# Sums of squares added elementwise first, key squares in column groups, split products for the values, and a shared key copy in a two-layer hybrid decoder step

## What is computed

```python
cq, ckv, kr = split(rms_norm(x, norm_g) @ w_in)        # 512 | 256 | 32 channels
q = rms_norm((rms_norm(cq, q_a_norm) @ w_uq).reshape(B, T, 16, 96), q_norm)
c = rms_norm(ckv, kv_a_norm)
k_nope = einsum('btc,chd->bthd', c, w_uk)              # 16 heads x 64
ssq = sum(square(k_nope), -1) + sum(kr * kr, -1)[..., None]
inv_r = rsqrt(ssq / 96 + EPS)                          # a scale per token and head
v = einsum('btc,chv->bthv', c, w_uv)                   # 16 heads x 64
```

## Time and profile before

| | |
|---|---|
| median of three executions | 1514.9 us |
| lowest, highest | 1511.93 us, 2867.42 us |
| span of the profiled execution | 1503.7 us |
| TensorE busy in it | 1457.7 us (97%) |
| VectorE, ScalarE, GpSimd busy | 756.1, 595.4, 162.6 us |

### The profile page before, as it was taken

The page is one execution under the profiler, slowest core; times in us unless marked ns, Lnnn a source line. Parts: engine busy times, 40 slices in busy tenths (PEclk is TensorE's granted clock), DMA queues, the critical chain, the costliest instruction groups (busy, mean ns, idle before and its releaser), DMA issues.

```text
span 1503.7 us, 29069 instructions
## 1 busy us (share of the span) xinstructions
PE 1457.7 (97%) x11768; PEld 1366.1 (91%) x11768; DVE 756.1 (50%) x1284; ACT 595.4 (40%) x909; POOL 162.6 (11%) x194
## 2 busy tenths in 40 slices
PE   7999988889999999999999999999999999999999
PEld 6999988877999999999999967655799999999999
DVE  6887555667964444443323327566444444443222
ACT  5444532334344344332223364567434434432111
POOL 1000022211810000000100000452020000000000
PEclk9999999999999999999999999999999999999999
DMA  5222200003452232333333420465323222333232
GB/s 216 85 84 84 85 1 29 29 29 105 148 193 95 88 94 84 98 88 103 101 91 90 113 85 29 144 195 167 115 85 94 89 96 86 87 94 91 88 91 81
DMA packets 48575, 144.64 MB, mean 96 GB/s; under 512 B 6912, under 2 KB 16224, under 8 KB 47344
## 3 DMA queue, kind: packets, MB, share of 16 engines
q1 hardware_dynamic: 42048, 118.57, 25.4%
q0 software_dynamic: 6160, 20.79, 4.6%
q10 hardware_dynamic: 288, 4.19, 0.7%
HBM read 134.73 MB, written 7.76 MB: 95 GB/s over the span
## 4 chain that ended last, share of the span: by engine, by line
PE 86%; DVE 7%; issue 3%; ACT 2%; DVEq 0%; DMA 0%; ACTq 0%; POOLq 0%
PE PS L561 85%; DVE arena L1837 2%; ACT arena L1633 1%; PE PS L1094 1%; DVE arena L2000 1%; DVE mx L2275 1%; DVE arena L1827 0%; DVE arena L1832 0%; ACT wsplit L1276 0%; DVE arena L2052 0%; DVE wsplit L1739 0%; DMA gains<-in_gains 0%; DVE arena L1835 0%; ACT arena L1455 0%; DVE arena L2027 0%
## 5 line engine op out<-in xcount | busy, mean ns | idle before, releaser
L561 PE MATMUL PS<-xnh,wsplit 128*128 128x260 f32 x3904 | 636.8, 284 | 12.6 <-DVE wsplit L1739 12.6
L561 PEld LDWEIGHTS PS<-xnh,wsplit 128*128 128x128 f32 x3904 | 539.5, 189 | 15.1 <-DVE wsplit L1739 13.2
L561 PE MATMUL PS<-xnl,wsplit 128*128 128x260 f32 x1952 | 393.7, 283 | 0.0
L1276 ACT ACTIVATE wsplit<-wring 128x1024 fp32r<-128x1024 f32 x176 | 183.0, 1040 | 438.1 <-PE PS L561 434.8
L1739 DVE TENSOR_TENSOR wsplit<-wring,wsplit 128x1024 fp32r<-128x1024 f32 x176 | 211.0, 1199 | 207.1 <-ACT wsplit L1276 207.0
L561 PEld LDWEIGHTS PS<-xnl,wsplit 128*128 128x128 f32 x1952 | 301.2, 189 | 0.0
L561 PE MATMUL PS<-hidh,wsplit 128*128 128x260 f32 x1408 | 226.6, 283 | 0.0
L561 PEld LDWEIGHTS PS<-hidh,wsplit 128*128 128x128 f32 x1408 | 192.9, 188 | 0.0
L561 PE MATMUL PS<-arena 128*128 128x128 f32 (+9 forms) x1104 | 170.9, 322 | 13.1 <-DVE arena L2000 8.6
L561 PEld LDWEIGHTS PS<-arena 128*128 128x128 f32 (+2 forms) x1104 | 134.3, 191 | 48.2 <-issue 30.1
L561 PE MATMUL PS<-hidl,wsplit 128*128 128x260 f32 x704 | 141.3, 282 | 0.0
(11 more groups left out here) (411 smaller groups left out, 1649.9 us busy)
## 6 DMA issues: line engine op xcount, KB each, us to landing
wring<-in_w_gu SPq DMA_DIRECT2D x88, 512.0 KB, 3.6
wring<-in_w_dn SPq DMA_DIRECT2D x32, 512.0 KB, 3.5
wring<-in_w_proj SPq DMA_DIRECT2D x28, 512.0 KB, 3.6
wring<-in_w_dn SPq DMA_DIRECT2D x16, 384.0 KB, 3.1
wring<-in_w_outa SPq DMA_DIRECT2D x8, 512.0 KB, 4.1
wring<-in_w_inc SPq DMA_DIRECT2D x8, 512.0 KB, 3.6
wring<-in_w_uq SPq DMA_DIRECT2D x8, 512.0 KB, 4.9
wring<-in_w_outc SPq DMA_DIRECT2D x8, 512.0 KB, 3.9
```

Source lines behind the costliest of these rows:

```text
L561: return pe.matmul(out, lhsT, rhs, start=start, stop=stop)
L1276: act.activation(dst[:, 0:w], wring[slot(stage, u)][:, 0:w], ACT.Copy).then_inc(s('w_hi'), 1)
```

## The change

- **Norms:** all eight squares of a norm are added elementwise; `norm_sum` has one `both`. The eighth add is GpSimd's in norms 1 to 3. In norm 0 it is VectorE's, behind `low('proj', 0, 1)`.
- **Latent squares:** VectorE adds the two squares of the keys' latent, GpSimd the four of the queries' (`add_latent`), and TensorE sums over partitions once for each group. The sum for the queries moves to behind key tile 2.
- **Key squares:** ScalarE's squares of four tiles are kept in four buffers. `key_squares(t)` sums each of the four into its own group of 32 PSUM partitions, after tile 5 (t=0) and after tile 7 (t=1). The sum is copied to `sq` by ScalarE and gathered to 16 rows by one more `both`, after the second value output; the key's root moves there too.
- **Values:** their weights are split (high part on GpSimd, remainder on VectorE behind the last key copy) and they are computed in 48 fp32r products of 512 columns.
- **Key copies:** VectorE copies the odd head of each key tile (`key_copy`), and ScalarE waits for that copy before it squares the tile and copies the even head.

```diff
-            for k in range(first, KD - 1):
+            for k in range(first, KD):
                 add_square(n, k)
...
             pool.dma_start(O['rows_c'], clat).then_inc(s('out_stored'), 16)
+            add_latent(2)
+            add_latent(3)
             pool.wait_ge(s('rot_ready'), 5)
...
+            add_latent(4)
+            add_latent(5)
+            for k in range(2):
+                pool.wait_ge(w_loaded[k], 16 * (GBASE['uq'] + 1))
+                pool.tensor_copy(uvh[:, k, :], wring[k][:, :]).then_inc(s('rest_hi'), 1)
...
+            pool.wait_ge(s('v_mm'), 8)
             pool.dma_start(wukt, A['w_ukt']).then_inc(g_loaded, 16)
...
-                pe.wait_ge(s('sq_added'), (KD - 1) * (n + 1))
-                both(4, const('ones_d'), sqsum, True, False)
-                pe.wait_ge(s('sq_ready'), KD * (n + 1))
-                both(4, const('ones_d'), sq[:, 1, :], False, True).then_inc(s('ssq_mm'), 1)
+                pe.wait_ge(s('sq_added'), squares_before(n) + KD)
+                both(4, const('ones_d'), sqsum).then_inc(s('ssq_mm'), 1)
...
-            mean_square(0)
-            mean_square(1)
+            pe.wait_ge(s('sq_added'), KD * 3 + 1)
+            both(4, const('ones_256'), sq[:, 0, :]).then_inc(s('latent_mm'), 1)
             latent_tile(3)
...
             latent_tile(4)
-            pe.wait_ge(s('rot_ready'), 4)
-            mean_square(2)
-            mean_square(3)
             latent_tile(5)
...
+            def key_squares(t):
+                pe.wait_ge(s('kn_sq'), 4 * t + 4)
+                for half in range(2):
+                    for g in range(4):
+                        ins = mm(PS[32 * g:32 * g + 32, 4 + half, 0:HALF], const('keysel')[:, 32 * t:32 * t + 32],
+                                 squares[g][:, half * HALF:(half + 1) * HALF], t == 0, t == 1)
+                ins.then_inc(s('kn_mm'), 1)
...
-                if m == 0:
-                    mean_square(4)
-                if m == 1:
-                    mean_square(5)
-                if m >= 1:
-                    key_square(m - 1)
-            key_square(7)
+                if m == 2:
+                    pe.wait_ge(s('rot_ready'), 4)
+                    pe.wait_ge(s('sq_added'), KD * 3 + 5)
+                    both(6, const('ones_512'), sqsum).then_inc(s('latent_mm'), 1)
+                if m == 5:
+                    key_squares(0)
+            key_squares(1)
...
+            pe.wait_ge(s('rest_split'), 3)
...
-                    ins = mm(PS[:, 6 + n % 2, :], clat[:, k, (n // 2) * 128:(n // 2 + 1) * 128],
-                             wring[k][:, (n % 2) * 512:(n % 2 + 1) * 512], k == 0, k == 1)
+                    mm(PS[:, 6 + n % 2, :], clh[:, k, toks], uvh[:, k, ns_], k == 0, False)
+                    mm(PS[:, 6 + n % 2, :], cll[:, k, toks], uvh[:, k, ns_], False, False)
+                    ins = mm(PS[:, 6 + n % 2, :], clh[:, k, toks], uvl[:, k, ns_], False, k == 1)
...
+                if n == 1:
+                    pe.wait_ge(s('kn_sq'), 9)
+                    both(4, const('keysel')[:, 64:64 + MH], sq[:, 0, :], True, False)
+                    pe.wait_ge(s('c_hi'), 1)
+                    both(4, const('ones_96')[0:32, 0:16], krsq, False, True).then_inc(s('kn_mm'), 1)
...
             def key_tile(m):
...
-                act.wait_ge(*((s('kn_mm'), m - 1) if m >= 2 else (s('cq_mm'), 5 + m)))
-                act.activation(two(sq[:, p, :]), bank2(2 * p), ACT.Square).then_inc(s('kn_sq'), 1)
-                for e in range(2):
...
+                act.wait_ge(*((s('kn_mm'), 1) if m >= 4 else (s('rot_ready'), 5) if m >= 2 else (s('sq_added'), KD * 3 + 4 + m)))
+                act.wait_ge(s('key_copied'), m + 1)
+                act.activation(two(squares[m % 4]), bank2(2 * p), ACT.Square).then_inc(s('kn_sq'), 1)
+                act.activation(two(khat[0:64, 2 * m, :]), PS[0:64, 2 * p:2 * p + 2, 0:HALF], ACT.Copy).then_inc(tile_taken[p], 1)
             for m in range(8):
                 key_tile(m)
-                if m == 1:
-                    act.wait_ge(s('cq_mm'), 6)
+                if m == 2:
+                    act.wait_ge(s('latent_mm'), 4)
                     rsqrt(R_CQ, two(rinv[:, R_CQ % 2, :]), bank2(6))
-                if 3 <= m <= 6:
-                    act.wait_ge(s('c_norm'), m)
-                    act.activation(cqh[:, m - 3, :], cqraw[:, m - 3, :], ACT.Copy).then_inc(s('c_hi'), 1)
+                if m >= 4:
+                    act.wait_ge(s('c_norm'), m - 1)
+                    act.activation(cqh[:, m - 4, :], cqraw[:, m - 4, :], ACT.Copy).then_inc(s('c_hi'), 1)
...
             low('proj', 0, 1)
+            square_added(KD - 1)
...
+            for m in range(3):
+                key_copy(m)
             dve.wait_ge(s('rinv_ready'), R_CQ + 1)
             for j in range(4):
+                key_copy(3 + j)
                 st(stt(out=cqraw[:, j, :], in0=cqraw[:, j, :], scalar=small[:, C_QA + j:C_QA + j + 1], in1=rinv[:, R_CQ % 2, :],
                        op0=ALU.mult, op1=ALU.mult), s('c_norm'))
                 if j:
                     latent_low(j + 1)
                 if j >= 2:
                     low('uq', 0, j)
+            key_copy(7)
+            for k in range(2):
+                dve.wait_ge(s('rest_hi'), 2 + k)
+                st(tt(uvl[:, k, :], wring[k][:, :], uvh[:, k, :].bitcast(F32), ALU.subtract), s('rest_split'))
             latent_low(5)
```

More of the change, by code:

```diff
@@ L74 @@
 CONSTS = ['ident', 'triu', 'decaymask', 'causal', 'ones', 'ones_d', 'ones_128', 'ones_256', 'ones_512',
-          'ones_96', 'rot128', 'sel4', 'headsel'] + [f'inv{l}' for l in range(LV + 1)]
+          'ones_96', 'rot128', 'sel4', 'keysel'] + [f'inv{l}' for l in range(LV + 1)]
 C_GDN, C_D, C_SSM, C_QA, C_KVA, C_QN, C_QR, C_KR, C_KN, C_EPS, C_QK, NSMALL = 0, 1, 5, 9, 13, 15, 16, 17, 18, 19, 20, 21
@@ L342, in s, with squares_before @@
             return sems[name]
+        def squares_before(n):
+            return KD * n + (5 if n == 3 else 0)
         def slot_freed(stage, i, u):
@@ L470, in add_square, with add_latent @@
                 else:
-                    pool.wait_ge(s('sq_added'), (KD - 1) * n + k)
+                    pool.wait_ge(s('sq_added'), squares_before(n) + k)
                     pool.tensor_tensor(sqsum[:, :], sqsum[:, :], sq[:, k % 2, :], ALU.add).then_inc(s('sq_added'), 1)
             def sum_squares(n, first=0):
-                for k in range(first, KD - 1):
+                for k in range(first, KD):
                     add_square(n, k)
+            def add_latent(j):
+                pool.wait_ge(s('cq_sq'), j + 1)
+                if j == 2:
+                    pool.tensor_copy(sqsum[:, :], sq[:, 0, :]).then_inc(s('sq_added'), 1)
+                else:
+                    pool.wait_ge(s('sq_added'), KD * 3 + j - 1)
+                    pool.tensor_tensor(sqsum[:, :], sqsum[:, :], sq[:, j % 2, :], ALU.add).then_inc(s('sq_added'), 1)
             pool.memset(raw[:, 0, 0:3], 0.0)
@@ L940, in latent_tile @@
                 ins.then_inc(gemm_ready[p], 1)
[L942 to L946, removed]
             latent_tile(0)
@@ L970, in _ @@
             pe.wait_ge(s('ln_ready'), R_KV + 1)
-            def key_square(m):
-                pe.wait_ge(s('kn_sq'), m + 1)
-                both(4, const('headsel')[:, m * 16:(m + 1) * 16], sq[:, m % 2, :], m == 0, False).then_inc(s('kn_mm'), 1)
+            def key_squares(t):
[5 more added lines that the diff above has]
+                ins.then_inc(s('kn_mm'), 1)
             for m in range(8):
@@ L980, in _ @@
                 ins.then_inc(gemm_ready[p], 1)
-                if m == 0:
-                    mean_square(4)
-                if m == 1:
-                    mean_square(5)
-                if m >= 1:
-                    key_square(m - 1)
-            key_square(7)
-            pe.wait_ge(s('c_hi'), 1)
-            both(4, const('ones_96')[0:32, 0:16], krsq, False, True).then_inc(s('kn_mm'), 1)
-            for u in range(2):
-                pe.wait_ge(w_loaded[u], 16 * (GBASE['uq'] + 1))
+                if m == 2:
[6 more added lines that the diff above has]
+            pe.wait_ge(s('rest_split'), 3)
             pe.wait_ge(s('ln_ready'), R_CQ + 1)
@@ L1529, in latent_square @@
                 if j >= 2:
-                    act.wait_ge(s('cq_mm'), j - 1)
+                    act.wait_ge(*((s('latent_mm'), 2) if j < 4 else (s('sq_added'), KD * 3 + j - 2)))
                 src = clat[:, j, :] if j < 2 else cqraw[:, j - 2, :]
@@ L1588, in _ @@
                 if t < 4:
-                    act.wait_ge(*((s('kn_mm'), 8) if t < 2 else (s('rot_ready'), 5)))
+                    act.wait_ge(s('kn_mm'), 3)
                 else:
@@ L2169, in _ @@
             latent_out(1)
-            dve.wait_ge(s('kr_mm'), 1)
+            dve.wait_ge(s('cq_sq'), 2)
+            st(tt(sq[:, 0, :], sq[:, 0, :], sq[:, 1, :], ALU.add), s('sq_added'))
+            dve.wait_ge(s('latent_mm'), 1)
```

(12 more changed lines are left out.)

35 lines of the change are left out of this document (20 added, 15 removed).

## The result

The changed kernel takes **1513.47 us** in the median (1504.72 to 1515.84, 20 runs), the kernel before on the same chip 1507.36 us (20 runs from 1504.05, with one of 2867). The ratio is 1.0026, 95% interval 1.0013 to 1.0038: slightly slower, well within 2%. The first three times of before gave 11.2 us between span and run; 20 runs show 1.7 (a run of 1515.35 us had a span of 1513.6). Against the kernel before I had forecast -1.4 us, and it is about +3.9 (0.26%).

The account below looks back on a forecast made before the run. TensorE was taken as the bound, with ScalarE also nearly full in the key phase. Norm 0 +1.25, norms 1 and 3 -1.74, norm 2 to queries -0.87 gave -1.4: span 1502.3 plus 11.2, 1513.5 us; 8-in-10 range 1506 to 1519.

Parts of the forecast that it names:

- the sum: Whole kernel: norm 0 +1.25, norms 1 and 3 -1.74, norm 2 to the queries -0.87, together -1.4 us.
- Norm 0: Norm before the convolution: VectorE's eighth add waits behind a weight remainder, so TensorE goes on later, +1.25 us.
- Norms 1 and 3: Each loses one `both` of 0.87 us, with GpSimd's eighth add covered: -1.74 us together.
- norm 2 and the single latent sum: Norm 2 loses one `both`, and the keys' latent pair of sums becomes one: -0.87 us each.
- Norm 2 to the queries: Norm 2 through key phase and values: earlier savings mostly eaten by the key-phase chain, -0.87 us left.
- The walk: Key-phase queues followed tile by tile: VectorE and ScalarE tied together, TensorE idle, values start at 881.3 against 880.99.
- The copy at 0.70 us: Key phase: VectorE's 64x520 copy out of PSUM priced at 0.70 us, with 0.42 as the other end.
- Values: 48 fp32r products of 512 columns at 0.225 us each; phase ends at 894.1 against 894.99.
- A: Rival: TensorE sets the pace and the saving shows in full, -14.2 us, 1500.7; chance 0.12.
- B: Rival: split-value products take 0.34 us each, costing more than plain ones, +4.0 us, 1518.9; chance 0.13.
- C: Rival: GpSimd operations around key phase and norms hold up VectorE's, +2.8 us, 1516.3; chance 0.10.
- Span to run time: Whole kernel: 11.2 us added between the profile's span of 1502.3 and the median run time.

Follow-up runs that it names:

- e1: Changed kernel with norm 0 alone summed as before the change (seven adds on VectorE, two sums on TensorE): 1511.53 us, ratio to before 1.0023.
- e9: e6 with the values in plain fp32 as before, without the rounded copies and remainders: 1505.52 us.
- e4: Changed kernel with VectorE's key-phase queue reordered, key copies and value-weight remainders earlier, same instructions: 1503.09 us, ratio to before 0.9967.
- e6: Changed kernel with e1 and e4 together: 1499.33 us, ratio to before 0.9946.
- e2: Changed kernel with 14 unread fp32 products of 260 columns filling TensorE's key-phase idle ahead of the second key_squares: 1509.79 us, ratio to before 1.0011.
- e10: e2 plus 16 unread products of 128 columns in norm 0's wait, so both new idles are filled: 1512.35 us.
- e5: Changed kernel with 26 unread products of 256 columns laid between the thin ones at the start of attention: 1511.14 us, ratio to before 1.0018.
- the series: Kernel before with 2, 4, 8, 12 or 20 unread products of 260 columns ahead of the values: 1509.96, 1513.59, 1510.99, 1514.67, 1517.34 us.
- e8: e6 with six unread dense products at the start of attention: 1499.68 us, ratio to before 0.9937.
- e13: Kernel before with 20 unread products of 260 columns ahead of the values: 1517.34 us.

## Why the prediction failed

- **Direction, wrong: -1.4 forecast, +3.9 measured.** The step that failed is the sum: it priced TensorE's idle by its length alone and carried no term for the granted clock. The first paragraph read that clock as at the upper level "in nearly every slice" and then left it out. What the runs show in its place: work -2.8, low clock +6.4. What the change moves was right to about 1 us a part, and the low clock outweighed it.
- **Norm 0, +1.25:** right as work (1.26, e1). The total at 151 us is +3.04; the missing 1.8 is the clock after the idle.
- **Norms 1 and 3, -1.74:** -0.93 and -0.86, right; norm 2 and the single latent sum, -0.73 and -0.79 against 0.87 each.
- **Norm 2 to the queries, -0.87:** measured +0.2 (from +1.67 to +1.88). The walk gave the tile times to within 1 us, shifted by the 1.67 us that after is late at norm 1: key phase from 854.93 (walk 853.2, shifted 854.9), last copy at 878.93 (walk 879.9). It was 0.9 too late at that copy, and 1.8 short of the low clock behind it (0.8 in the key squares, 1.0 in the first value products). The copy at 0.70 us is exact. What the prediction took from the Trainium skill, "VectorE: DVE Perf Modes", section "Why PSUM operands drop a tier", that an fp32 operand in PSUM keeps VectorE at its plain rate, agrees with it: 0.70 us for 520 columns out of PSUM, where the copy within SBUF took 0.42.
- **Values:** 0.2315 us for a product against 0.225; 11.1 against 14.0 us in all, confirmed by e9.
- **Everything behind the queries** stood in the sum as unchanged, without a word. It is the largest error of the profiled run: +7.3 us at the start of attention and +1.55 by 1090, all of it clock.
- **Rivals:** A did not happen as run, but e4 and e6 show that most of it was there behind VectorE's order (work -9.0 for e6). B is refuted. C's mechanism is there once, off the chain. Beside a GpSimd add of 1.75 us, VectorE's line 2212 took 1.69 us, where the same operation in the kernel before, with GpSimd at rest, took 0.69. GpSimd's copy took longer too, 3.13 us beside VectorE's remainders and 0.78 in the norms. TensorE shows no idle there. The first three lines are of after, the fourth of before, the fifth is a group of after:

```profile
846.91 3.13 POOL L487 COPY sqsum<-sq 128x520 f32<-128x520 f32 x1
850.19 1.75 POOL L490 TENSOR_TENSOR sqsum<-sqsum,sq 128x520 f32<-128x520 f32 x1
850.80 1.69 DVE L2212 TENSOR_TENSOR arena<-arena 32x520 f32<-32x520 f32 x1
...
850.72 0.69 DVE L2188 TENSOR_TENSOR arena<-arena 32x520 f32<-32x520 f32 x1
...
L474 POOL COPY sqsum<-sq 128x520 f32<-128x520 f32 x3 | 2.3, 778 | 50.5 <-ACT sq L1279 50.5
```

- **Span to run time:** 1.7 us, not 11.2. That error and the missing clock cancelled in the forecast number.

**What stays open.** Shown: the two new idles bring the clock down (e1, e2, e10), VectorE's order caused most of the idle of the key phase (e4), and in the changed kernel dense work at the start of attention brings the share down (e5). Not shown: why a clock of 0.988 or less comes in four of five runs of the changed kernel and its near kin, and in one of five before. It isn't the earlier low stretches (e10), nor a shift alone as far as the series goes. Kernels with the copies first (e4, e6, e8, e9) have 17 of 42, in between. The 7.3 us of the profiled run are located, their trigger is not known. The Trainium skill, "TensorE: Matmul & The Clock Gate", in its Part 1 on the clock gate, says that the gate's view of the engine's activity runs free of the kernel's start. The traces agree: at norm 0, where after, e2, e4 and e5 run the same instructions and the idle starts at 18.7 to 18.9 us, the clock falls at 21.0, 21.9, 20.7 and 21.9. That this also decides how long the start of attention is low would fit the moments given above, and no experiment shows it.

## What to carry to other kernels

An idle of TensorE in the midst of dense work can cost more than its length: look up the granted clock of the windows behind it, and put the next products at half speed into the upper end of the price (here 1.8 us for each of two idles). When products are removed from a phase, order the other engines' queues first by who releases TensorE's buffers; here this alone turned 0.3% slower into 0.3% faster. If two kernels differ by less than their own runs do, compare runs at like clocks, and don't take one profile's distance for that of the medians.

## What the hardware showed

- TensorE's clock went to the lower level right behind idles of 1.98 us (norm 0), 1.96 us with shorter ones ahead of it (e6) and 6.24 us (key phase); filled with products, it did not. Not every such idle does this: behind 1.94 us (e4) and 1.96 us (e9) at the same place as e6's it stayed up, and behind one of 3.32 us at 201 to 205 us it fell in 15 of 16 profiles (not in e13).
- It also fell while TensorE was never idle for more than 0.35 us, in work with many products of 1 and 16 columns (before, at 961.1).
- A VectorE operation on 32 rows of 520 in SBUF took 1.69 us beside a GpSimd add of 1.75 us, and 0.69 with GpSimd at rest.
- With identical code and data the time of a run varies by some 11 us with the clock granted: 1504.7 to 1515.8 us for the changed kernel.
- A product of 512 columns took 0.2315 us in fp32r (one pass) and 0.875 in fp32 (two records of 0.4375 each).
